# Moving the split hidden activations by 128 bytes against the output weights, on one core

## Chip, cores and metric

One core of a Trainium2 chip runs the whole program in one launch. The metric is the device time of that launch in microseconds. The matrix engine (TensorE) is PE in the profile, the vector engine DVE, the scalar engine ACT, GpSimd POOL, the engine that issues most transfers SP.

## The reference, cut to what matters

256 tokens of width 1024 pass through three blocks one after the other. The first has two layers and the second one layer, each of them with a gated feed-forward before and after a mixer; the third has four layers, each with a mixer and a squared-ReLU feed-forward. All of it is in float32.

```python
def swiglu(x, w_gu, w_down):              # first block; the second is alike, width 2816
    g, u = jnp.split(x @ w_gu, 2, axis=-1)
    return (jax.nn.silu(g) * u) @ w_down

def squared_relu_mlp(xn, w_up, w_down):   # third block, width 4096
    return jnp.square(jax.nn.relu(xn @ w_up)) @ w_down
```

## The kernel before, in words

**Split numbers.** A float32 operand of a matmul is held as two float32r tiles, a high half (a copy that rounds) and a low half (the rest), and a product is three matmuls: high with high, high with low, low with high. ACT makes the high half of each weight unit from its landing buffer (`split_hi`), DVE the low half (`split_lo`), each in rings of two.

**A feed-forward** (class `FeedForward`) goes through its hidden width in units: 22 units of 128 columns in a gated stage (six such stages, 132 units), 16 units of 256 columns in a squared-ReLU stage (four stages, 64 units). For each unit PE runs `_hidden` (weights `in_hi`, `in_lo` stationary, normed activations `feat` moving), and then `_down` of the unit before it: the activations `hid_hi`, `hid_lo` are stationary, 128 columns at a time, and the output weights `down_hi`, `down_lo` move, 512 columns at a time, into four PSUM banks that accumulate over all units. `_down` is three groups: L1302 (`hid_hi` with `down_hi`), L1306 (`hid_hi` with `down_lo`), L1310 (`hid_lo` with `down_hi`), of 4 matmuls each in a gated unit and 8 in a squared-ReLU unit. The last unit of a stage runs the same products by `_last_down` (L1324, L1329, L1334). Every matmul has a weight load of its own. A turn of the loop has two units.

**The mixers** project by `Linear.block` (L1640, L1641, L1645): here `feat` is stationary and the weights `in_hi`, `in_lo` move, 512 columns at a time. Some of their projections (L2173 to L2175, L3110 to L3115) are turned round: weights stationary, `feat` moving, 256 columns.

**Where tiles lie.** `Core.__init__` lays all tiles out in SBUF one after the other. Its helper `phase(name, at)` puts in an unused tile, so that the next address equals `at` modulo `PERIOD` (256 bytes); `NEAR` is 64 bytes. With the address of `in_hi` as origin, the code gives these remainders modulo 256: `in_hi`, `in_lo` and `ring_in` 0; `feat` 0; `feat_near` and `feat2_hi`, `feat2_lo` -64; `proj` -64, and with it the tiles that lie over it: `ring_down`, `hid_hi`, `hid_lo`; `arena` -64, and with it `down_hi`, `down_lo`. Gated stages read the activations at -64 (in four of the six stages; two stages of the second block use rows 258 wide that alternate between -64 and +64). Squared-ReLU stages read `feat` at 0 and have their low weights `in_lo_near` at +64. All chunks inside a tile are whole multiples of 256 bytes apart, but for those wide rows.

I call the remainder of the moving operand's address less that of the stationary operand's the offset of a matmul. Before the change it is 0 for all of `_down`, L1207 too; -64 in L1209, L1210, L1217, L1216; 0 in the projection of the convolution mixer; +64 in the first blocks of the last stick-breaking projection (it reads `feat_near`), and -64 in its turned blocks; 0 in the turned block of the sliding-window mixer.

**The order of the work** is each engine's own list, with semaphores between them; SP loads the next unit into a ring when DVE has made the low half of the unit two before. `proj` itself holds the mixers' projections; attention reads parts of it as a matmul operand (L1816, L2046, L2731).

Of the kernel before, what the change touches and what calls it, by code (L numbers as in the profile page):

```python
# [31 lines left out]
PERIOD = 256  # L32
NEAR = 64
# [109 lines left out]
class Core:  # L143


    def __init__(self, nc, ctx, dram):
        self.nc, self.dram = nc, dram

        def sb(name, *shape):
            return ctx.enter_context(nc.sbuf_tensor(name, [P, *shape], F32))  # L150
# [7 lines left out]
        def phase(name, at):  # L158

            gap = (at - nc.sbuf_base) % PERIOD  # L160
            if gap:
                sb(name, gap // 4)
# [13 lines left out]
        at_in = nc.sbuf_base  # L176
# [8 lines left out]
        self.fold = sb("fold", TT, P)  # L185
        self.minus_half = sb("minus_half", 8)
        self.eps = sb("eps", 8)
        phase("hidden_gap", at_in - NEAR)
        at = nc.sbuf_base
        self.proj = sb("proj", TT, PROJ_COLS)  # L190

# [4525 lines left out]
```

## Time and profile before

| | |
|---|---|
| median of 3 runs | 2865.47 us (2858.51 to 2865.72) |
| the profiled execution | 2865.0 us, its span 2863.2 us |
| PE busy | 2766.1 us, 97% of the span |
| DVE, ACT, POOL busy | 1944.9, 1195.1, 610.4 us |
| mean granted clock | 0.984 |

A matmul's length in the profile holds its latency, and the next one starts before it ends. What a matmul costs in a dense stretch is therefore the distance between two starts, which I call its pitch, and not its length: a row of the timeline gives the start of a run of equal matmuls, and the difference of two starts, divided by the matmuls between them, is the pitch. Starts are rounded to 0.01 us.

### The profile page before, as it was taken

How to read it: one execution, taken by the hardware profiler on the slowest of the kernel's cores; microseconds unless marked ns; L12 is line 12 of the kernel's file. 1: busy time of each engine (PE TensorE's matmuls, PEld its weight loads, DVE VectorE, ACT ScalarE, POOL GpSimd, SP SyncE). 2: the span in 40 equal slices, each digit the busy share in tenths (PEclk: the TensorE clock that was granted, in tenths of full speed). 3: DMA queues.
4: the chain of work that ended last, by engine and by line, in shares of the span. 5: the costliest groups of instructions: out<-in, count | busy, mean ns of one | idle time of the engine just before them, and what ended most of it. 6: DMA issues, size and time to landing. Idle time of an engine off the chain costs nothing.

```text
span 2863.2 us, 43965 instructions
## 1 busy us (share of the span) xinstructions
PE 2766.1 (97%) x17384; PEld 2446.3 (85%) x17384; DVE 1944.9 (68%) x2181; ACT 1195.1 (42%) x1468; POOL 610.4 (21%) x513
## 2 busy tenths in 40 slices
PE   8999999999999999999999999999999989999998
PEld 7987789989978998998789898888788878888887
DVE  7985665678866986664666656666766657665665
ACT  4343443333353343334443445434443444345433
POOL 5953310048533971000100000000000320000000
PEclk9999999999999999999999999999999999999999
DMA  7654135457535674443344343544554335533542
GB/s 288 259 185 158 53 126 191 184 210 255 209 104 186 255 262 176 178 161 103 118 181 178 140 162 155 205 176 154 185 204 176 120 123 215 196 134 119 210 191 105
DMA packets 126465, 500.31 MB, mean 175 GB/s; under 512 B 11024, under 2 KB 12336, under 8 KB 92960
## 3 DMA queue, kind: packets, MB, share of 16 engines
q1 hardware_dynamic: 112768, 450.39, 43.0%
q0 software_dynamic: 13600, 48.60, 4.9%
q8 instruction: 65, 1.06, 0.2%
q14 instruction: 32, 0.26, 0.0%
HBM read 497.90 MB, written 1.05 MB: 174 GB/s over the span
## 4 chain that ended last, share of the span: by engine, by line
PE 74%; DVE 13%; issue 6%; ACT 3%; DMA 2%; POOL 2%; DVEq 0%; SPq 0%; ACTq 0%; POOLq 0%
PE duo L1207 8%; PE duo L1302 7%; PE duo L1306 6%; PE duo L1310 6%; PE duo L1209 6%; PE duo L1210 6%; PE duo L1217 6%; PE duo L1216 4%; DVE down_lo L360 4%; PE duo L1640 3%; PE duo L1641 3%; PE duo L1645 3%; DVE in_lo L360 2%; DVE hid_hi L1466 2%; DMA ring_in<-in_ffn_in 2%
## 5 line engine op out<-in xcount | busy, mean ns | idle before, releaser
L360 DVE TENSOR_TENSOR in_lo<-ring_in,in_hi 128x2048 fp32r<-128x2048 f32 x295 | 704.9, 2390 | 293.4 <-ACT in_hi L353 293.2
L353 ACT CAST in_hi<-ring_in 128x2048 fp32r<-128x2048 f32 (+1 forms) x293 | 554.8, 1894 | 265.1 <-PE duo L1645 137.9
L360 DVE TENSOR_TENSOR down_lo<-ring_down,down_hi 128x1024 fp32r<-128x1024 f32 (+1 forms) x196 | 370.2, 1889 | 29.5 <-ACT down_hi L353 29.5
L353 ACT CAST down_hi<-ring_down 128x1024 fp32r<-128x1024 f32 (+1 forms) x196 | 260.5, 1329 | 45.4 <-PE duo L1310 44.6
L1302 PE MATMUL duo<-down_hi,hid_hi 128*128 128x512 f32 x984 | 258.5, 394 | 10.5 <-DVE hid_hi L1466 9.3
L1209 PE MATMUL duo<-feat,in_hi 128*128 128x256 f32 (+1 forms) x1056 | 258.6, 285 | 5.2 <-ACT in_hi L353 3.4
L1210 PE MATMUL duo<-feat,in_hi 128*128 128x256 f32 (+1 forms) x1056 | 256.4, 283 | 0.0
L1306 PE MATMUL duo<-down_lo,hid_hi 128*128 128x512 f32 x984 | 254.5, 390 | 0.0
L1310 PE MATMUL duo<-down_hi,hid_lo 128*128 128x512 f32 x984 | 253.3, 389 | 0.0
L1207 PE MATMUL duo<-feat,in_hi 128*128 128x512 f32 x1024 | 250.8, 395 | 0.0
L1207 PEld LDWEIGHTS duo<-feat,in_hi 128*128 128x128 f32 x1024 | 191.3, 188 | 46.5 <-DVE feat L655 6.0
L1005 POOL TENSOR_TENSOR small<-small,minus_half 128x1 f32<-128x1 f32 x16 | 8.8, 552 | 1006.3 <-DVE small L1038 1006.0
L1306 PEld LDWEIGHTS duo<-down_lo,hid_hi 128*128 128x128 f32 x984 | 185.3, 188 | 39.8
L1310 PEld LDWEIGHTS duo<-down_hi,hid_lo 128*128 128x128 f32 x984 | 185.0, 188 | 38.6
L1375 ACT ACTIVATE act<-act 128x256 f32<-128x256 f32 x88 | 36.8, 418 | 423.4 <-DVE act L1433 423.3
L1209 PEld LDWEIGHTS duo<-feat,in_hi 128*128 128x128 f32 x1056 | 201.9, 191 | 11.5 <-ACT in_hi L353 3.7
L3312 POOL TENSOR_TENSOR mod_sum<-mod_sum,mod_w 128x1024 f32<-128x1024 f32 x63 | 206.9, 3285 | 5.3
L1302 PEld LDWEIGHTS duo<-down_hi,hid_hi 128*128 128x128 f32 x984 | 172.3, 189 | 39.0 <-ACT down_hi L353 11.0
L1210 PEld LDWEIGHTS duo<-feat,in_hi 128*128 128x128 f32 x1056 | 202.0, 191 | 2.2
L1382 ACT CAST hid_hi<-act 128x512 fp32r<-128x512 f32 x64 | 39.7, 620 | 347.6 <-DVE act L1481 347.6
L1640 PE MATMUL duo<-in_hi,feat 128*128 128x512 f32 x432 | 173.7, 402 | 0.2 <-DVE feat L655 0.2
L1641 PE MATMUL duo<-in_hi,feat 128*128 128x512 f32 x432 | 170.5, 395 | 0.0
(522 smaller groups left out, 5508.2 us busy)
## 6 DMA issues: line engine op xcount, KB each, us to landing
ring_in<-in_ffn_in SPq DMA_DIRECT2D x196, 1024.0 KB, 6.1
ring_down<-in_ffn_down SPq DMA_DIRECT2D x132, 512.0 KB, 3.5
ring_down<-in_ffn_down SPq DMA_DIRECT2D x64, 1024.0 KB, 4.8
mod_w<-in_w_ada POOLq DMA_DIRECT2D x72, 512.0 KB, 4.8
ring_in<-in_sb_w_qkv SPq DMA_DIRECT2D x24, 1024.0 KB, 5.1
ring_in<-in_conv_w_in SPq DMA_DIRECT2D x12, 1024.0 KB, 5.1
ring_in<-in_gla_w_in SPq DMA_DIRECT2D x12, 1024.0 KB, 5.1
ring_in<-in_nsa_w_in SPq DMA_DIRECT2D x10, 1024.0 KB, 5.1
```

The source lines that it names most:

```text
L353: act.copy(hi[:, s, 0:n], raw[:, s, 0:n]).then_inc(hi_ready.sem, 1)
L360: dve.tensor_tensor(lo[:, s, 0:n], raw[:, s, 0:n], hi[:, s, 0:n].bitcast(F32), ALU.subtract).then_inc(lo_ready.sem, 1)
L1207: pe.matmul(out.rearrange("p (s n) -> p s n", s=2), hi, k.feat[:, :, c, :], start=opens, stop=False, skip_group_check=True)
L1209: pe.matmul(out, hi, self.feat_hi[:, c, :], start=opens, stop=False, skip_group_check=True)
L1210: pe.matmul(out, hi, self.feat_lo[:, c, :], start=False, stop=False, skip_group_check=True)
L1217: return pe.matmul(out, lo, self.feat_hi[:, c, :], start=False, stop=(c == KC - 1), skip_group_check=True)
L1302: pe.matmul(self.acc(t, n), hid_hi, down_hi, start=first and ch == 0, stop=False)
L1306: pe.matmul(self.acc(t, n), hid_hi, down_lo, start=False, stop=False)
L1310: last = pe.matmul(self.acc(t, n), hid_lo, down_hi, start=False, stop=False)
L1640: pe.matmul(out, self.feat_hi[:, 4 * h + c, tok], w_hi[:, c, :], start=(h == 0 and c == 0), stop=False)
L1641: pe.matmul(out, self.feat_lo[:, 4 * h + c, tok], w_hi[:, c, :], start=False, stop=False)
L3312: pool.tensor_tensor(total, total, mod.w[:, s, :], ALU.add).then_inc(mod.used.sem, 1)
```

## The change

The unused tile ahead of `proj` is sized so that `proj`, and with it `ring_down`, `hid_hi` and `hid_lo`, lie at +64 instead of -64. The tile ahead of `arena` is still sized for -64, so `down_hi` and `down_lo` keep their remainder. The offset of the matmuls of `_down` and `_last_down` goes from 0 to -128, which modulo 256 is +128. No instruction is added, removed or moved in order.

```diff
         self.fold = sb("fold", TT, P)
         self.minus_half = sb("minus_half", 8)
         self.eps = sb("eps", 8)
-        phase("hidden_gap", at_in - NEAR)
+        phase("hidden_gap", at_in - NEAR + PERIOD // 2)
         at = nc.sbuf_base
         self.proj = sb("proj", TT, PROJ_COLS)
```

## Rows read from the trace of the kernel before

**Rows 1.** The page: span, busy us of each engine, granted TensorE clock in 40 slices:

```profile
span 2863.2 us, 43965 instructions
...
PE 2766.1 (97%) x17384; PEld 2446.3 (85%) x17384; DVE 1944.9 (68%) x2181; ACT 1195.1 (42%) x1468; POOL 610.4 (21%) x513
...
PEclk9999999999999999999999999999999999999999
```

**Rows 2.** The page: chain that ended last, shares of the span by engine:

```profile
PE 74%; DVE 13%; issue 6%; ACT 3%; DMA 2%; POOL 2%; DVEq 0%; SPq 0%; ACTq 0%; POOLq 0%
```

**Rows 3.** PE groups by form: count, busy us, mean ns of one, idle before:

```profile
L1302 PE MATMUL duo<-down_hi,hid_hi 128*128 128x512 f32 x984 | 258.5, 394 | 10.5 <-DVE hid_hi L1466 9.3 <-ACT hid_hi L1382 1.1
...
L1306 PE MATMUL duo<-down_lo,hid_hi 128*128 128x512 f32 x984 | 254.5, 390 | 0.0
...
L1310 PE MATMUL duo<-down_hi,hid_lo 128*128 128x512 f32 x984 | 253.3, 389 | 0.0
...
L1324 PE MATMUL duo<-down_hi,hid_hi 128*128 128x512 f32 x56 | 19.8, 400 | 0.0
...
L1207 PE MATMUL duo<-feat,in_hi 128*128 128x512 f32 x1024 | 250.8, 395 | 0.0
...
L1816 PE MATMUL duo<-arena,proj 128*64 128x256 f32 x112 | 18.7, 413 | 2.1 <-DVE feat L3948 1.5 <-DVE feat L1936 0.7
```

**Rows 4.** Timeline of PE, half a turn of a squared-ReLU stage: start, length, count:

```profile
1801.13 3.83 PE L1207 MATMUL duo<-feat,in_hi 128*128 128x512 f32 x16
...
1804.80 2.05 PE L1216 MATMUL duo<-feat,in_lo 128*128 128x256 f32 x16
...
1806.69 1.99 PE L1302 MATMUL duo<-down_hi,hid_hi 128*128 128x512 f32 x8
...
1808.51 1.98 PE L1306 MATMUL duo<-down_lo,hid_hi 128*128 128x512 f32 x8
...
1812.14 3.83 PE L1207 MATMUL duo<-feat,in_hi 128*128 128x512 f32 x16
```

**Rows 5.** Timeline of PE, half a turn of a gated stage:

```profile
505.05 2.05 PE L1217 MATMUL duo<-feat_hi,in_lo 128*128 128x256 f32 x16
...
506.93 1.09 PE L1302 MATMUL duo<-down_hi,hid_hi 128*128 128x512 f32 x4
...
507.86 1.07 PE L1306 MATMUL duo<-down_lo,hid_hi 128*128 128x512 f32 x4
...
509.68 0.28 PE L1209 MATMUL duo<-feat_hi,in_hi 128*128 128x256 f32 x1
```

**Rows 6.** Timeline of PE, convolution mixer's projection, 12 matmuls apart:

```profile
1948.10 1.07 PE L1645 MATMUL duo<-in_lo,feat 128*128 128x512 f32 x4
...
1950.82 1.07 PE L1645 MATMUL duo<-in_lo,feat 128*128 128x512 f32 x4
```

**Rows 7.** Timeline of PE, last stick-breaking projection, 12 matmuls apart:

```profile
2563.35 1.08 PE L1645 MATMUL duo<-in_lo,feat 128*128 128x512 f32 x4
...
2566.10 1.08 PE L1645 MATMUL duo<-in_lo,feat 128*128 128x512 f32 x4
```

**Rows 8.** Timeline of PE, the first gated stage's first unit:

```profile
25.10 1.98 PE L1217 MATMUL duo<-feat,in_lo 128*128 128x256 f32 x16
...
26.91 1.09 PE L1302 MATMUL duo<-down_hi,hid_hi 128*128 128x512 f32 x4
```

**Rows 9.** Timeline of PE, same projection later, 108 matmuls apart:

```profile
2573.56 0.28 PE L2173 MATMUL duo<-feat,in_hi 128*128 128x256 f32 x1
...
2585.80 0.28 PE L2173 MATMUL duo<-feat,in_hi 128*128 128x256 f32 x1
```

**Rows 10.** Timeline of PE, sliding-window mixer's projection, 7 matmuls apart:

```profile
790.18 0.28 PE L3110 MATMUL duo<-feat,in_hi 128*128 128x256 f32 x1
...
791.02 0.28 PE L3111 MATMUL duo<-feat,in_hi 128*128 128x256 f32 x1
```

**Rows 11.** Timeline of DVE, same half turn as rows 5, idle time in brackets:

```profile
507.13 0.42 DVE L1433 TENSOR_TENSOR act<-duo,y 128x256 f32<-128x256 f32 x1 [2.17 <-PE duo L1217]
```
## What I predict, and why

> **What bounds the kernel now.** I read the page first. PE is busy for 2766.1 of 2863.2 us, DVE for two thirds, and the granted clock is the higher level (2.4 GHz) in nine tenths or more of every slice [rows 1]. The chain of work that ended last lies on PE for 74% [rows 2]; the reader should see that no other engine has a share near it. So PE's own pace sets the time, and an edit that adds no instruction can only act through that pace or through a wait that is not there yet.
>
> The groups by form come next. The products with the output weights are 984 matmuls in each of three groups and 56 more in each of the three groups of the last units, for which L1324 stands [rows 3], so 3 x 984 + 3 x 56 = 3120 matmuls with 512 moving columns. PE was idle ahead of them for 10.5 us in all, nearly all of it for `hid_hi` from DVE [rows 3]. Their mean lengths differ though their forms are the same: 394, 390 and 389 ns in order of execution [rows 3]. That is the first sign that their pace has a history.
>
> Then the timeline, read for pitch. In the squared-ReLU half turn, 8 matmuls L1302 take 1806.69 to 1808.51, 227.5 ns each, and the 16 after them 1808.51 to 1812.14, 226.9 ns each. The 16 of L1207 take 1801.13 to 1804.80, 229.4 each [rows 4]. In the gated half turn 4 matmuls L1302 take 0.93 us, 232.5 ns each, and the 8 after them 1.82 us, 227.5 each [rows 5]. At the higher clock 512 columns alone are 512 / 2.4 = 213.3 ns. The reader should see a floor near 226.7 ns, and that a group entered from another one first pays some extra and then settles at the floor.
>
> What the settled pitch depends on shows in two projections with the same form and the same code. At offset 0 twelve matmuls take 1948.10 to 1950.82, 226.7 ns each [rows 6]. At offset +64 twelve take 2563.35 to 2566.10, 229.2 ns each [rows 7]. The second never reaches the floor. So 64 bytes cost 2.5 ns per matmul with 512 columns. With 256 columns there are three paces: 113.3 ns at offset -64 over 108 matmuls [rows 9] and 113.1 in the first unit [rows 8]; 117.5 ns at the same offset -64 in a gated unit after a `_down` [rows 5]; and 120 ns at offset 0, 0.84 us for 7 [rows 10]. So a pace belongs to an offset and to what ran before. The offset modulo 512 seems not to matter: by the code `down_hi` less `hid_hi` is 256 modulo 512, `in_hi` less `feat` is 0, and both settle at the floor [rows 4, 6].
>
> **The change part by part.**
>
> *Addresses.* From `in_hi` to `hidden_gap` are 59,200 bytes, 64 modulo 256. Before, both unused tiles were 128 bytes. Now `proj` wants +64 and is already there, and it is 24,704 bytes long, 128 modulo 256, so it ends at -64, where `arena` wants to begin. Both unused tiles vanish: `proj` and the tiles over it move down by 128 bytes, `arena` and all behind it by 256, which keeps its remainders.
>
> *What it takes away.* The extras that `_down` pays today until it settles. Gated unit: 4 x 232.5 + 8 x 227.5 = 2750 ns less 12 x 226.7 = 2720, so 30 ns, times 132 units is 4.0 us [rows 5]. Squared-ReLU unit: 8 x 0.8 ns and 16 x 0.2, 10 ns, times 64 is 0.6 us [rows 4]. At most these 4.6 us can be saved in `_down`. L1207, which follows `_down`, pays 16 x 2.7 = 43 ns a unit today, 2.8 us in all; that depends on how `_down` leaves PE, and could go either way.
>
> *What it adds.* A price on each of the 3120 matmuls. The trace has no stretch of such matmuls that I can place at offset 128. Bounds: nothing, if it settles as offset 0 does [rows 6]; and 120 - 113.3 = 6.7 ns, the largest gap between two paces of one form [rows 9, 10]. The nearest row is +64 with 2.5 ns [rows 7]. The offset is twice as far from 0, and 256 columns also show more price with more than one step, so I take twice the price of one step, 5.0 ns, as an estimate. 3120 x 5.0 = 15.6 us; less the 4.6 that this price replaces, 11.0 us. At the bounds: 3120 x 6.7 - 4.6 = +16.3 us, and 0 - 4.6 = -4.6 us. One step's price would give 3120 x 2.5 - 4.6 = +3.2 us.
>
> *What I cost at nothing.* DVE's second subtraction reads `ring_down` and `down_hi`, which now lie 128 apart. What hides it is DVE's idle time before the next instruction, 2.17 us in a gated half turn [rows 11]. If it took longer than that, `hid_hi` would be late, and L1302 is queued behind it. The casts of ACT are hidden in the same way. Attention reads parts of `proj` as operands; L1816 has 112 such matmuls with 256 columns [rows 3], and at 6.7 ns either way these are 0.8 us. I leave that out of the sum and in the range. The transfers are the same in number and size, and `arena` moves by a whole period.
>
> The sum is 2865.0 + 11.0 = 2876.0 us for the profiled execution. Its 2865.0 agrees with the median 2865.5, so the forecast for the median is 2876, which is 0.4% slower.
>
> **The rivals.**
>
> *No effect, or one cheap step.* Offset 128 may settle like 0, or cost what 64 costs: 2860 to 2869 us. For it: offset 0 does settle, and a price that repeats every 128 bytes fits the two 512-column offsets in the trace as well as one that repeats every 256. Against it: nothing in the trace shows such a repeat. The Trainium skill (SBUF — State Buffer, "Who interferes with whom") goes further: PE has two independent read ports, one for the moving operand and one for the weight load, and PE never waits on anyone. By that rule addresses don't matter at all, and the kernel would stay at 2865 us. The trace does not agree: the same form at two offsets has 226.7 and 229.2 ns [rows 6, 7].
>
> *Faster: the hidden products fall into their fast pace.* The 256-column matmuls at -64 have two paces, 113.3 and 117.5 ns [rows 9, 5]. The first unit, which no `_down` precedes, has the fast one [rows 8]; a later unit, entered from a `_down` that had settled, has the slow one [rows 5]. The stretch of rows 9 followed a block at +64 that never settled [rows 7], and was fast. If `_down` at 128 leaves PE as that block did, the four gated stages with 256 columns save 4 x 22 x 48 x 4.2 ns = 17.7 us. With a price of 2.5 ns in `_down` (+3.2) the result is 2865 - 14.5 = 2850 us. With 5.0 ns (+11.0) it is 2858. Against it: one case of an entry is no rule, and at the full 6.7 ns in `_down` (+16.3) it decides nothing any more. The rival wins by over 0.3% only where `_down` pays less than about 4.4 ns: 3120 x 4.4 - 4.6 = 9.1, and 17.7 - 9.1 = 8.6 us.
>
> *Slower by more.* The new exit of `_down` brings the hidden products to the 120 ns pace: 88 x 48 x 2.5 ns = 10.6 us on top, 2887 us. The price of 6.7 ns alone gives 2881.
>
> **How the numbers follow.** A measurement of this kernel can tell about 0.3%, 8.6 us, from no change. My forecast (5 ns, hidden pace kept, 2876) has a chance of 0.36. Slower by more (2881 to 2887 and above) has 0.12. No effect or one cheap step (2860 to 2869) has 0.32, of which 0.10 for addresses that don't matter here at all. The fast hidden pace has 0.20: 0.16 near 2850 and lower, 0.04 near 2858, which is counted as the same. So slower 0.48, same 0.36, faster 0.16. The range for 8 in 10 runs from 2848, which takes in the fast pace with one cheap step, to 2887, the worse exit. The forecast case alone has 2871 to 2881.
>
> **What would show it.** In the changed kernel's timeline, the pitch of L1306 and L1310 settled above 226.7 ns, near 231.7, or cycling as at +64, shows the price; 226.7 refutes it. L1302 no longer dearer than the two behind it shows that the entry's extra was replaced. L1209, L1210 and L1217 still at 117.5 ns shows that the hidden pace was kept; 113.3 is the faster rival, 120 the slower one. L1207 at 229.4 shows its entry unchanged. DVE's and ACT's times per instruction should stay, and PE's idle time ahead of L1302 near 10.5 us; growth there would mean that the cost came through a wait and not through the pace. My forecast is wrong if the price at 128 is not further along from that at 64, or if what follows `_down` changes its pace; both rest on an extrapolation from two offsets, and the sum has nothing better.

## The result, and the profile after

| | before | after |
|---|---|---|
| median of 20 runs each | 2865.59 us (2858.51 to 2875.41) | 2871.84 us (2865.17 to 2877.36) |
| ratio | | 1.0021, 95% interval 1.0014 to 1.0029 |
| profiled execution | 2865.0 us, span 2863.2 | 2869.8 us, span 2868.0 |

The kernel became 0.21% slower. The interval leaves out 1, so this is a real cost, but it is under the 0.3% that the prediction counts as no difference. The instructions stand in the same order on every engine, so the two traces can be laid over each other.

The page of the kernel after, span, busy times, granted clock, and the chain that ended last by engine:

```profile
span 2868.0 us, 43965 instructions
...
PE 2768.1 (97%) x17384; PEld 2434.3 (85%) x17384; DVE 1945.5 (68%) x2181; ACT 1196.8 (42%) x1468; POOL 613.5 (21%) x513
...
PEclk9999999999999999999999999999999999999999
...
PE 71%; DVE 15%; issue 7%; ACT 4%; DMA 2%; POOL 2%; DVEq 0%; SPq 0%; ACTq 0%; POOLq 0%
```

The granted clock is the higher level (2.4 GHz) in nine tenths or more of every slice, as before [rows 1]. That does not clear the clock altogether: its mean differs a little between executions, and the account over all kernels below takes that up. PE's busy time rose by 2.0 us only. The chain says more: PE's share of it fell from 74% [rows 2] to 71%, DVE's rose from 13% to 15%. That suggests that something was gained on PE and something lost to DVE.

The groups of PE by form, after (count, busy us, mean ns, idle before):

```profile
L1302 PE MATMUL duo<-down_hi,hid_hi 128*128 128x512 f32 x984 | 261.5, 397 | 13.5 <-DVE hid_hi L1466 12.4 <-ACT hid_hi L1382 1.0
L1306 PE MATMUL duo<-down_lo,hid_hi 128*128 128x512 f32 x984 | 260.2, 396 | 0.0
L1310 PE MATMUL duo<-down_hi,hid_lo 128*128 128x512 f32 x984 | 259.4, 395 | 0.0
```

Against [rows 3] the three groups of `_down` are 3, 6 and 6 ns longer, and the idle time ahead of L1302 grew from 10.5 to 13.5 us.

The timeline of PE after: a unit of a gated stage with 256 columns (503 to 512 us), a unit that follows a wait (128 to 140), and a unit of a squared-ReLU stage (1815 to 1822):

```profile
128.69 1.98 PE L1217 MATMUL duo<-feat,in_lo 128*128 128x256 f32 x16
...
130.87 1.18 PE L1302 MATMUL duo<-down_hi,hid_hi 128*128 128x512 f32 x4 [0.20 <-DVE hid_hi L1466]
...
137.50 2.05 PE L1217 MATMUL duo<-feat,in_lo 128*128 128x256 f32 x16
139.39 1.09 PE L1302 MATMUL duo<-down_hi,hid_hi 128*128 128x512 f32 x4
...
503.70 1.09 PE L1302 MATMUL duo<-down_hi,hid_hi 128*128 128x512 f32 x4
...
506.49 0.28 PE L1209 MATMUL duo<-feat_hi,in_hi 128*128 128x256 f32 x1
...
510.13 1.98 PE L1217 MATMUL duo<-feat_hi,in_lo 128*128 128x256 f32 x16
511.95 1.09 PE L1302 MATMUL duo<-down_hi,hid_hi 128*128 128x512 f32 x4
...
1815.80 2.02 PE L1302 MATMUL duo<-down_hi,hid_hi 128*128 128x512 f32 x8
...
1821.38 3.83 PE L1207 MATMUL duo<-feat,in_hi 128*128 128x512 f32 x16
```

Three things are to be read here.

1. *`_down` pays and never settles.* Gated: 503.70 to 506.49 are 12 pitches, 232.5 ns each, against 229.2 before [rows 5]. Squared-ReLU: 1815.80 to 1821.38 are 24 pitches, 232.5 ns each, against 227.1 before [rows 4]. That is 1584 x 3.3 + 1536 x 5.4 ns = +13.5 us. (It takes all gated units at the price of those with 256 columns. In the 528 matmuls of the 258-column stages the median pitch went from 227.6 to 233.0 ns, which makes the sum 1.1 us larger.)
2. *The hidden products after it became faster.* 510.13 to 511.95 is 113.8 ns per matmul; it was 117.5 [rows 5]. The 48 hidden products of a unit take 506.49 to 511.95, 5.46 us; with a unit of 8.40 us before, of which `_down` took 2.75, they took 5.65. That is 88 x 0.19 = -16.7 us. The length of the L1217 group shows the pace at a glance: 1.98 us is fast, 2.05 us slow [rows 8, 5].
3. *The fast pace can be lost.* At 130.87 L1302 waits 0.20 us for DVE, and the hidden products behind it are slow: 137.50 to 139.39, 118.1 ns each. The next unit is fast again. In the profiled execution 5 of the first 66 gated units ran slow.

The distance between the starts of two L1310 groups is the length of a unit. Its median for each kind of stage, worked out from all starts of the two timelines:

```
                        units   before   after   difference x units
gated, 256 columns        88     8.40     8.25     -13.2 us
gated, 258 columns        44     8.50     8.56      +2.6 us
squared-ReLU              64    11.01    11.13      +7.7 us
                                              sum   -2.9 us
```

By the median unit of each kind the kernel should have become 2.9 us faster. It became 6.0 us slower, by the ratio. The missing 9 us are not in the pitch of the ordinary unit. The waits of PE, after:

```profile
PE duo L1302 <- DVE hid_hi L1466: 12.4, 11, 2.3
```

Before, this wait had 9.3 us [rows 3]. The timeline of DVE after shows where it comes from, a quiet unit at 513 us and a disturbed one from 621 us on:

```profile
513.59 0.29 DVE L1466 CAST hid_hi<-act 128x256 fp32r<-128x256 f32 x1
...
514.94 2.29 DVE L360 TENSOR_TENSOR in_lo<-ring_in,in_hi 128x2048 fp32r<-128x2048 f32 x1 [0.59 <-ACT in_hi L353]
517.14 1.22 DVE L360 TENSOR_TENSOR down_lo<-ring_down,down_hi 128x1024 fp32r<-128x1024 f32 x1
...
621.96 2.19 DVE L1466 CAST hid_hi<-act 128x256 fp32r<-128x256 f32 x1
...
624.57 3.66 DVE L360 TENSOR_TENSOR in_lo<-ring_in,in_hi 128x2048 fp32r<-128x2048 f32 x1
628.15 3.41 DVE L360 TENSOR_TENSOR down_lo<-ring_down,down_hi 128x1024 fp32r<-128x1024 f32 x1
```

And GpSimd's timeline over the same stretch:

```profile
621.60 2.41 POOL L3312 TENSOR_TENSOR mod_sum<-mod_sum,mod_w 128x1024 f32<-128x1024 f32 x1
...
626.16 4.31 POOL L3312 TENSOR_TENSOR mod_sum<-mod_sum,mod_w 128x1024 f32<-128x1024 f32 x1
```

The cast of 0.29 us takes 2.19 us while GpSimd's addition runs from 621.60 to 624.01. The two subtractions behind it are lengthened as well, DVE has no idle time up to 631.9 us, and the next `hid_hi` comes 1.44 us too late for PE at 635.32. The Trainium skill (SBUF — State Buffer, "Who interferes with whom") says that DVE and GpSimd share a pair of ports, and that the one that comes second is blocked for the other's whole instruction. The times here agree with it: the cast ends at 624.15, just after the addition at 624.01, and the second subtraction at 631.56, about 1.1 us after the next addition at 630.47; 1.22 us is its length alone.

### The profile page after: what moved, and what is told of

The parts are those of the page before. It is cut to its first block, busy times and chain, and to the rows that moved or that the text cites. A ratio compares the mean times of both kernels' runs of the same rounds, so it can differ in the third digit from the quotient of the medians.

```text
span 2868.0 us, 43965 instructions
## 1 busy us (share of the span) xinstructions
PE 2768.1 (97%) x17384; PEld 2434.3 (85%) x17384; DVE 1945.5 (68%) x2181; ACT 1196.8 (42%) x1468; POOL 613.5 (21%) x513
## 4 chain that ended last, share of the span: by engine, by line
PE 71%; DVE 15%; issue 7%; ACT 4%; DMA 2%; POOL 2%; DVEq 0%; SPq 0%; ACTq 0%; POOLq 0%
PE duo L1207 8%; PE duo L1302 6%; PE duo L1306 6%; PE duo L1310 6%; PE duo L1209 5%; PE duo L1210 5%; PE duo L1217 5%; DVE down_lo L360 5%; PE duo L1216 4%; PE duo L1640 3%; PE duo L1641 3%; PE duo L1645 3%; DVE in_lo L360 3%; DVE hid_hi L1466 2%; DMA ring_in<-in_ffn_in 2%
## 5 line engine op out<-in xcount | busy, mean ns | idle before, releaser
L1302 PE MATMUL duo<-down_hi,hid_hi 128*128 128x512 f32 x984 | 261.5, 397 | 13.5 <-DVE hid_hi L1466 12.4
L1306 PE MATMUL duo<-down_lo,hid_hi 128*128 128x512 f32 x984 | 260.2, 396 | 0.0
L1310 PE MATMUL duo<-down_hi,hid_lo 128*128 128x512 f32 x984 | 259.4, 395 | 0.0
L1209 PE MATMUL duo<-feat,in_hi 128*128 128x256 f32 (+1 forms) x1056 | 253.9, 283 | 5.1 <-ACT in_hi L353 3.4
L1210 PE MATMUL duo<-feat,in_hi 128*128 128x256 f32 (+1 forms) x1056 | 251.6, 281 | 0.0
L1207 PE MATMUL duo<-feat,in_hi 128*128 128x512 f32 x1024 | 250.9, 395 | 0.0
L1207 PEld LDWEIGHTS duo<-feat,in_hi 128*128 128x128 f32 x1024 | 191.2, 188 | 47.1 <-DVE feat L655 6.0
L1306 PEld LDWEIGHTS duo<-down_lo,hid_hi 128*128 128x128 f32 x984 | 186.6, 190 | 44.3
L1310 PEld LDWEIGHTS duo<-down_hi,hid_lo 128*128 128x128 f32 x984 | 185.9, 189 | 43.5
L1302 PEld LDWEIGHTS duo<-down_hi,hid_hi 128*128 128x128 f32 x984 | 172.4, 189 | 42.9 <-ACT down_hi L353 13.2
```

Of the source, the lines that this page charges most:

```text
L1207: pe.matmul(out.rearrange("p (s n) -> p s n", s=2), hi, k.feat[:, :, c, :], start=opens, stop=False, skip_group_check=True)
L1209: pe.matmul(out, hi, self.feat_hi[:, c, :], start=opens, stop=False, skip_group_check=True)
L1210: pe.matmul(out, hi, self.feat_lo[:, c, :], start=False, stop=False, skip_group_check=True)
L1302: pe.matmul(self.acc(t, n), hid_hi, down_hi, start=first and ch == 0, stop=False)
L1306: pe.matmul(self.acc(t, n), hid_hi, down_lo, start=False, stop=False)
L1310: last = pe.matmul(self.acc(t, n), hid_lo, down_hi, start=False, stop=False)
```

## The experiments

The kernel before is the base of every kernel and every ratio.

**1. The hid tiles alone.** `ring_down`, `proj` and `arena` stay at their remainders.

```diff
-        at += 4 * RING * UNIT
+        at += 4 * RING * UNIT + PERIOD // 2
```

> Only hid_hi and hid_lo move by 128 bytes; proj, ring_down and arena stay where they were before. Theory (the price comes from the remainder of each matmul's two operands): the same as the full change, ratio 1.001 to 1.003 to the kernel before, L1306 and L1310 at a pitch of about 232 ns, L1209 and L1217 of a gated unit at 113.3. Rival (it comes from the landing ring, the projections or the arena, which moved as well): ratio 1.000, pitches 226.7 and 117.5.

Measured 2869.69 us against 2864.54, ratio 1.0024 (1.0014 to 1.0034). The pitches are those of the change, units of 8.25, 8.56 and 11.13 us too. The whole effect belongs to the tiles that `_down` loads as weights.

**2. Everything but the hid tiles.** The edit of the change, and the hid tiles shifted back.

```diff
-        phase("hidden_gap", at_in - NEAR)
+        phase("hidden_gap", at_in - NEAR + PERIOD // 2)
...
-        at += 4 * RING * UNIT
+        at += 4 * RING * UNIT + PERIOD // 2
```

> The complement: proj and ring_down move by 128 bytes and arena by 256 as in the full change, but hid_hi and hid_lo keep their old remainder against down_hi and down_lo. Theory: ratio 1.000 to the kernel before, pitches 226.7 (L1306, L1310) and 117.5 (L1217), DVE's and ACT's times per instruction as before. Rival (moved landing ring or arena): ratio 1.002.

Measured 2865.21 us, 1.0007 (0.9997 to 1.0017), with the pitches of before. `ring_down`, `proj` and `arena` cost nothing that can be measured.

**3. Only `hid_lo` shifted.** Only the last group of `_down`, L1310, has offset 128.

```diff
-        at += 4 * RING * 2 * TOKENS
+        at += 4 * RING * 2 * TOKENS + PERIOD // 2
```

> Only hid_lo moves by 128 bytes, so of the three groups only L1310, the last before the hidden products, has offset 128. Theory (the hidden products' pace is set by how the last group leaves PE): L1302 and L1306 near the floor of 226.7 ns after their entry, L1310 about 232, hidden products of gated units at 113.3; 1040 matmuls x 5.5 ns = 5.7 us paid, about 14 us of pitch gained, of which waits for DVE take back some: 2855 to 2862 against 2866 before, ratio 0.996 to 0.999. Rival (the pace follows the whole of the product, or hid_hi's place): hidden pace stays 117.5, ratio 1.002.

Measured 2870.57 us, 1.0023 (1.0014 to 1.0031). The timeline of PE, a gated unit and a squared-ReLU unit:

```profile
503.89 2.05 PE L1217 MATMUL duo<-feat_hi,in_lo 128*128 128x256 f32 x16
505.77 1.09 PE L1302 MATMUL duo<-down_hi,hid_hi 128*128 128x512 f32 x4
...
507.62 1.10 PE L1310 MATMUL duo<-down_hi,hid_lo 128*128 128x512 f32 x4
508.55 0.28 PE L1209 MATMUL duo<-feat_hi,in_hi 128*128 128x256 f32 x1
...
1820.43 1.98 PE L1306 MATMUL duo<-down_lo,hid_hi 128*128 128x512 f32 x8
1822.24 2.02 PE L1310 MATMUL duo<-down_hi,hid_lo 128*128 128x512 f32 x8
1824.11 3.82 PE L1207 MATMUL duo<-feat,in_hi 128*128 128x512 f32 x16
```

In the squared-ReLU unit L1310 has 1.87 us / 8 = 233.8 ns, and L1306 just ahead of it 226.3: the price switches with the offset, from one group to the next. But the hidden products stay slow (1.88 us / 16 = 117.5 ns). My theory that the offset of the last group alone decides their pace fell.

**4. Only `hid_hi` shifted.** L1302 and L1306 at 128, L1310 at 0.

```diff
-        at += 4 * RING * UNIT
+        at += 4 * RING * UNIT + PERIOD // 2
...
-        at += 4 * RING * 2 * TOKENS
+        at += 4 * RING * 2 * TOKENS + PERIOD // 2
```

> Only hid_hi moves by 128 bytes: L1302 and L1306 at offset 128, L1310 back at 0. Theory: 2080 matmuls x 5.5 ns = 11.4 us paid, less some 4 us of today's entry, plus a new entry at L1310; L1310 settles at 226.7 and hands over as before, so hidden products stay at 117.5: 2871 to 2877, ratio 1.002 to 1.004. Rival (hid_hi's place sets the hidden pace): 113.3 and a ratio near 1.000.

Measured 2869.88 us, 1.0017 (1.0004 to 1.0030). The timeline of PE:

```profile
505.39 1.09 PE L1310 MATMUL duo<-down_hi,hid_lo 128*128 128x512 f32 x4
506.32 0.28 PE L1209 MATMUL duo<-feat_hi,in_hi 128*128 128x256 f32 x1
...
509.95 1.98 PE L1217 MATMUL duo<-feat_hi,in_lo 128*128 128x256 f32 x16
...
1813.02 1.99 PE L1310 MATMUL duo<-down_hi,hid_lo 128*128 128x512 f32 x8
1814.84 3.83 PE L1207 MATMUL duo<-feat,in_hi 128*128 128x512 f32 x16
```

Here the fast hidden pace is there (L1217 in 1.98 us), though L1310 has the old offset. And L1310 doesn't settle in a gated unit: four matmuls in 0.93 us are 232.5 ns each, at offset 0. With eight of them, in the squared-ReLU unit, the mean is 227.5. So the price is not a property of the offset alone; a group carries on for a few matmuls what the group before it left. The last group's pitch does not tell the pace of the hidden products either: it is 232.5 ns in a gated unit of kernel 3, where they are slow, and of kernel 4, where they are fast. What they inherit from `_down` is thus neither the last offset nor the last pitch, and these two runs don't show what it is.

**5 and 6. Offsets +64 and -64.** This is kernel 5; kernel 6 has `at_in` alone there.

```diff
-        phase("hidden_gap", at_in - NEAR)
+        phase("hidden_gap", at_in + PERIOD // 2)
```

> proj, ring_down and the hidden tiles at +128, so all products with the output weights have offset +64; arena as before. Theory (the price of an offset in these products is that of the same offset in the projections): a pitch that cycles at 229.2 ns on average, 2.5 ns over the floor, 3120 x 2.5 - 4.6 = +3.2 us; if the gated units' hidden products are at 113.3 as after the last stick-breaking block, 10 us or so less, ratio 0.997; if they stay at 117.5, ratio 1.001. Rival (any offset but 0 costs about 5.5 ns here): 1.002 to 1.005.

> The same with offset -64 (hidden tiles at 0). No row of before has it with 512 columns. Theory: the price grows with the distance from 0 either way, so about as at +64: 229 ns, ratio 0.997 to 1.001 by the hidden pace. Rival (it grows in one direction, 0, 64, 128, 192): over 232 ns, 3120 x 7 - 4.6 = +17 us, ratio 1.006 with the hidden pace kept.

+64: 2871.08 us, 1.0018 (1.0006 to 1.0031). -64: 2874.66 us, 1.0033 (1.0021 to 1.0045). The timeline of PE at +64, a gated and a squared-ReLU unit:

```profile
506.04 1.07 PE L1302 MATMUL duo<-down_hi,hid_hi 128*128 128x512 f32 x4
...
508.79 0.28 PE L1209 MATMUL duo<-feat_hi,in_hi 128*128 128x256 f32 x1
...
1812.13 2.03 PE L1302 MATMUL duo<-down_hi,hid_hi 128*128 128x512 f32 x8
...
1817.73 3.81 PE L1207 MATMUL duo<-feat,in_hi 128*128 128x512 f32 x16
```

Gated: 2.75 us / 12 = 229.2 ns, the value of [rows 7]. Squared-ReLU: 5.60 us / 24 = 233.3 ns, with the same form, tiles and offset. So one offset has two paces, and something besides the offset chooses. At -64 it is 233.3 ns in both kinds of stage. Every offset but 0 brings the hidden products to the fast pace in most units (at -64 so many units of the first and the third stage ran slow or waited that their medians are 8.45 us, those of the other two are 8.24). Units at +64 are 8.20, 8.54 and 11.14 us.

**7 and 8. Before and after, with GpSimd's load cut.** GpSimd's multiplication and addition of the modulation weights run on 8 of 1024 columns, so these two kernels leave out nearly all of the modulation sums; transfers and instruction counts are kept.

```diff
-                k.pool_link(pool, pool.tensor_scalar(mod.w[:, s, :], mod.w[:, s, :], k.col("c_2", c), 0.0, ALU.mult, ALU.add))
+                k.pool_link(pool, pool.tensor_scalar(mod.w[:, s, 0:8], mod.w[:, s, 0:8], k.col("c_2", c), 0.0, ALU.mult, ALU.add))
...
-                pool.tensor_tensor(total, total, mod.w[:, s, :], ALU.add).then_inc(mod.used.sem, 1)
+                pool.tensor_tensor(total[:, 0:8], total[:, 0:8], mod.w[:, s, 0:8], ALU.add).then_inc(mod.used.sem, 1)
```

> The kernel before, with GpSimd's multiply and add of the modulation sums done on 8 columns in place of 1024 (so those sums are left out for the rest; transfers and semaphores are kept). DVE then should not be slowed beside it in the gated stages. Reference for the next run: some us faster than the kernel before, about 6 to 12 us, by fewer waits of PE for hid_hi.

> The same cut in the changed kernel (the same part of the modulation sums left out). Theory (the gated stages' faster hidden pace is given back as waits for a slowed DVE): with DVE free the gain shows in full, and the changed kernel is equal to or faster than its partner: 88 x -0.15 + 44 x 0.06 + 64 x 0.12 us = -2.9 us, ratio to the partner 0.998 to 1.000. Rival (the gain is lost elsewhere): still 1.002 to the partner.

Measured 2851.85 us, 0.9948 (0.9936 to 0.9959), and 2851.01 us, 0.9947 (0.9933 to 0.9961). The waits for `hid_hi` of the second one:

```profile
PE duo L1302 <- ACT hid_hi L1382: 1.0, 4, 0.3
```

DVE is gone from the list in both kernels, hardly a unit is longer than the median of its kind (0.2 us in all, against 20.0 us in the kernel after), and the 0.21% between them is gone too: their ratio is 0.9999. The intervals are wide (about 0.2% for the pair), so this supports that the loss needs GpSimd's load, but can't measure the 2.9 us that the pace alone should give. The two traces can: from the first L1310 of each feed-forward stage to its last, summed over the stages, kernel 8 takes 3.1 us less than kernel 7.

**9 to 11. Shift by kind of stage.** A gated unit fills only half of the columns of the hid tiles, so its views can start some columns in. Such a stage then has its own offset while no tile moves. In kernel 9 these are 48 columns, 192 bytes, which makes the offset -192, or +64 modulo 256.

```diff
+        self.hid_at = 3 * NEAR // 4 if silu and not self.shifted else 0
...
-        rows = slice(ch * TOKENS + t * P, ch * TOKENS + (t + 1) * P)
+        rows = slice(self.hid_at + ch * TOKENS + t * P, self.hid_at + ch * TOKENS + (t + 1) * P)
...
-        dve.tensor_tensor(k.hid_lo[:, j, 0:n], whole, hi.bitcast(F32), ALU.subtract).then_inc(k.hid_ready.sem, 1)
+        dve.tensor_tensor(k.hid_lo[:, j, self.hid_at:self.hid_at + n], whole, hi.bitcast(F32), ALU.subtract).then_inc(k.hid_ready.sem, 1)
```

The same slice stands wherever `hid_hi` is written. Kernel 10 has `2 * NEAR // 4` (offset 128) under the same condition. Kernel 11 moves the hid tiles as kernel 1 does and has `2 * NEAR // 4 if silu else 0`, so that only the squared-ReLU stages are at 128.

> Only the four gated stages with 256-column activations read and write their hidden halves 192 bytes further on in the ring slot (offset +64 to the output weights); squared-ReLU stages and the two wide gated stages keep offset 0, and no tile moves. Theory: unit of the narrow gated stages 8.20 us as with +64 everywhere, hidden products at 113.3, all other units as before (8.50, 11.01). 88 x 0.20 = 17.6 us of pitch gained, half of it or more given back to waits for DVE: 2855 to 2861, ratio 0.997 to 0.999, faster than both kernels. Rival (the gated gain is wholly lost to DVE): 1.000.

> The change's offset of 128 in the four narrow gated stages alone. Theory: their unit at 8.25 us as in the full change, the rest as before: 88 x 0.15 = 13.2 us of pitch gained, with half or more given back: ratio 0.998 to 0.9995. Rival (gated stages are slower by the change as well): over 1.000.

> Offset 128 in the four squared-ReLU stages alone (the hidden tiles at +64, the gated stages' views moved back to a remainder of -64); ring_down, proj and arena not moved. Theory: unit at 11.13 us against 11.01, 64 x 0.12 = 7.8 us slower, ratio 1.0027, gated units at 8.40 and 8.50. Rival (most of the loss is in the gated stages): near 1.001.

| | median us | ratio | interval |
|---|---|---|---|
| 9: narrow gated at +64 | 2861.06 | 0.9984 | 0.9971 to 0.9997 |
| 10: narrow gated at 128 | 2863.75 | 0.9985 | 0.9973 to 0.9998 |
| 11: squared-ReLU at 128 | 2872.73 | 1.0026 | 1.0010 to 1.0042 |

The change is thus two opposite effects: -0.15% in the four gated stages with 256 columns, +0.26% in the squared-ReLU stages. With the +0.1% that the wide stages should cost by their units (2.6 us; not run alone) they make +0.2%, the result. Kernels 9 and 10 are faster than both kernels of this case. But neither gains what its units say, 17.6 and 13.2 us.

**12. Kernel 9 with GpSimd's load cut.** It leaves out what kernels 7 and 8 leave out. If waits take all that is missing, the full gain must appear.

> Offset +64 in the narrow gated stages together with the light GpSimd (the same part of the modulation sums left out), to be read against the kernel before with light GpSimd, 0.9948 of the kernel before. Theory (waits for a slowed DVE take back what the pace gains): the 88 x 0.20 = 17.6 us now show in full or nearly, 2834 to 2840 us, 0.9885 to 0.991 of the kernel before, that is 0.994 to 0.996 of its partner. Rival (something else takes the gain back): 0.993 to 0.9945 of the kernel before, as the 5 us seen with GpSimd at its full work.

Measured 2844.51 us (2833.13 to 2851.86), 0.9932 (0.9914 to 0.9951). Against kernel 7, by the two ratios, that is 0.16% or 4.6 us, with an interval of some 6 us either way (7.3 us by the medians, whose bases differ by 1.7), and not 17.6. The theory's 0.9885 to 0.991 lies outside the interval, and the rival's range holds: the waits don't explain what is missing. The timeline of PE in the second gated stage:

```profile
410.75 2.05 PE L1218 MATMUL duo<-feat_hi,in_lo 128*128 128x256 f32 x16
412.63 1.09 PE L1303 MATMUL duo<-down_hi,hid_hi 128*128 128x512 f32 x4
...
414.50 1.10 PE L1311 MATMUL duo<-down_hi,hid_lo 128*128 128x512 f32 x4
```

The hidden products are slow (117.5 ns) and `_down` is dear (1.87 us / 8 = 233.8 ns), through the second and the third stage (44 units, 8.46 us at the median), while the first and the fourth have the fast pair (units of 8.20 us). The second stage of kernel 9 has the fast pair from end to end, the timeline of its PE:

```profile
481.58 1.08 PE L1303 MATMUL duo<-down_hi,hid_hi 128*128 128x512 f32 x4
...
483.41 1.08 PE L1311 MATMUL duo<-down_hi,hid_lo 128*128 128x512 f32 x4
...
487.97 1.98 PE L1218 MATMUL duo<-feat_hi,in_lo 128*128 128x256 f32 x16
489.78 1.07 PE L1303 MATMUL duo<-down_hi,hid_hi 128*128 128x512 f32 x4
```

Same addresses, same order, two states: 228.8 with 113.1 ns, or 233.8 with 117.5. With no wait for DVE to disturb it, PE stayed in the worse one for two stages, which is 44 x 0.26 = 11 us. That is most of the missing amount: the stages of this kernel take 5.6 us less than those of kernel 7 in the traces, as 44 x -0.20 + 44 x 0.06 = -6.2 us says. It may also be the reason for the wide spread of this kernel's runs: two of its executions with the same mean granted clock, 0.986, took 2844.91 us (the profiled one, with two slow stages) and 2833.13 us. Only the first has a trace, so that the other ran with fewer slow stages is not shown. In kernels 9 and 10 too some narrow gated units ran slow or waited, so many that the median of the fourth stage of kernel 9 is 8.41 us, and those of the first and the fourth stage of kernel 10 are 8.44.

**The account over all kernels.** All figures are in us, against the kernel before. Pace is the sum of the differences of unit medians by kind, times their units, as if every unit ran at the median; measured is the ratio times 2865 us, and rest is measured less pace. "Above" is what units longer than the median of their kind hold in excess, in the one profiled execution of each, less the 13.8 us of the kernel before. "Clock" is explained below the table. "Left" is the rest less these two.

```
kernel                     pace    measured   rest    above    clock    left
2  all but hid tiles        0       + 2.0     + 2.0   + 0.6    + 0.7    + 0.7
3  hid_lo alone           + 6.5     + 6.6     + 0.1   - 4.2    + 0.9    + 3.4
11 squared-ReLU at 128    + 7.7     + 7.4     - 0.3   + 0.1    - 0.1    - 0.3
after                     - 2.9     + 6.0     + 8.9   + 6.2    + 1.7    + 1.0
1  hid tiles alone        - 2.9     + 6.9     + 9.8   +10.6    + 0.8    - 1.6
4  hid_hi alone           - 6.6     + 4.9     +11.5   + 6.8    + 0.9    + 3.8
5  +64                    - 7.5     + 5.2     +12.7   + 8.2    + 1.3    + 3.1
6  -64                    - 2.7     + 9.5     +12.2   + 9.5    - 0.1    + 2.8
9  narrow gated +64       -17.6     - 4.6     +13.0   +10.5    + 1.7    + 0.8
10 narrow gated 128       -13.2     - 4.3     + 8.9   + 5.7    + 1.5    + 1.7
```

The split is clear. Where the hidden products keep their slow pace, the pitches explain the time to 2 us, within intervals of some 3 to 5 us either way. Where they become fast, 9 to 13 us are given back, whatever else was moved, and 6 to 11 us of that stand in long units. In the kernel after, 4.8 of its 6.2 us are in units in which PE waits, and 1.5 in units that ran slow without a wait.

The clock is the other part. At the joints between the stages and in the mixers the granted clock falls to the lower level (1.2 GHz) for short stretches. Outside the feed-forward stages these add up to 88 us in the profiled execution of the kernel before, 72 us in that of kernel 1 and 103 us in that of kernel 5. In all 14 traces the time outside the stages is 1180 us plus half of the time at the lower level, to within 4 us. For example, the 1361 matmuls behind the first gated stage, in the kernel before and in kernel 10, whose tiles lie where they lay before (window, its length, busy us of PE, PEld, DVE, ACT and POOL, granted clock, DMA share, GB/s):

```profile
200.00:412.00 212.00, 196.93 (x1361) 164.08 (x1360) 126.37 (x220) 84.59 (x202) 53.59 (x97) 0.95 0.30 98
...
200.00:418.00 218.00, 201.26 (x1361) 169.19 (x1360) 126.21 (x219) 84.44 (x202) 53.57 (x97) 0.93 0.29 95
```

The second takes 6 us more. It has 30 us at the lower level and the first 20, half of which difference is 5 us.

The executions without a trace show it as well. The kernel after took 2865.5 to 2867.9 us in the five with a mean clock of 0.986 or 0.987, and 2873.4 to 2877.4 us in the four with 0.982. Over all kernels 0.001 of the mean clock goes with 2.2 us. The kernel after has a mean of 0.9840 over its executions, the kernel before 0.9848 over the 91 that were measured beside the experiments; these 0.0008 are 1.7 us, the value in the table; those of the numbered kernels are against the executions of the base measured beside them (all are estimates: the mean clock of 6 to 20 executions is itself uncertain by about 0.0005). Whether the change lowers the clock or chance did, the runs don't show.

## Why the prediction came out as it did

The forecast was 2876 us and the measurement 2871.84, inside the 2871 to 2881 given for the likeliest case. But the way there was not the forecast one: two steps failed, in opposite directions, and that the number came out is luck.

- **The price of `_down`.** Right in kind, a little too small. The estimate was 5.0 ns settled and +11.0 us net; the pitch is 232.5 ns, 5.8 over the floor, and the net is +13.5 us. Kernel 11 shows it alone: 64 units x 0.12 = 7.7 us, measured 7.4. It doesn't settle, and it takes the place of the entry's extra, as said.
- **Why 5.0.** "Twice the price of one step" was close by luck. Kernel 5 has 2.5 ns and 6.7 ns at one and the same offset +64, and -64 has 6.7. The price doesn't grow with the distance from 0; the row of [rows 7] showed one of two states.
- **"Hidden pace kept".** This step failed. The four gated stages with 256 columns fell into the fast pace, -16.7 us, by which the time of the likeliest case should have gone to 2859 or, with the measured price, to 2862. The rival had the right effect, the right stages and nearly the right size (17.7 us). Its condition was not exact: in kernel 3 the last group doesn't settle, and the hidden products stay slow.
- **"What I cost at nothing".** This failed too, and gave back a part of the step above: 6.2 us in long units, of which 4.8 in units in which PE waits. The cover of 2.17 us [rows 11] was read in a quiet half turn. In the others it was too small even before the change, which shows in the 9.3 us of waits for DVE [rows 3]. Beside GpSimd a cast takes 2.19 us instead of 0.29 and a subtraction 3.41 instead of 1.22, and there is no cover left. The prediction named the sign of it, the idle time ahead of L1302, which went from 10.5 to 13.5 us. The sum also had no term for the granted clock, which moves single executions by several us.
- **The rival's threshold.** It was to win where `_down` pays less than 4.4 ns. It paid 5.8, so it could not win by over 0.3%; but 17.7 us were counted as if all of it arrived. Kernel 9, where `_down` of the gated stages pays least, gets 4.6 us of 17.6.
- **No effect, one cheap step, addresses that don't matter.** All three are refuted. Kernels 1 and 2 part the tiles; kernel 3 switches the pitch from 226.3 to 233.8 ns between two neighbouring groups of one unit by nothing but an address. The Trainium skill gives PE two independent read ports and says that PE never waits on anyone (SBUF — State Buffer, "Who interferes with whom"). Read as a rule that addresses don't matter, that is not borne out here; whether another engine can hold PE up at its ports, no run here tests.
- **Neighbours.** L1207 keeps its mean length of 395 ns [rows 3], as said. `ring_down`, `proj` and `arena` cost nothing that can be measured, as said (kernel 2, at most 0.17%).

Shown: the price in `_down` by tile and by stage, the gain of the hidden products, and that 9 to 13 us are given back when these are fast. Shown in part: where that goes. Kernels 7 and 8 tie the loss to GpSimd's load, the waits for `hid_hi` grew by 3.1 us, single units or whole stages drop back to the slow pace, and executions with more time at the lower clock are longer. With these the account closes to 4 us, which is within the intervals; but the long units come from one execution of each kernel, and a remainder of that size would not be seen. Also open is what chooses the state when a stage begins. After offset 0 it is always the slow one but for single units, after other offsets mostly the fast one, and kernel 3 with its dear last group is slow. Whether one kernel changes its state between executions is not shown, since only one of each was profiled; the two executions of kernel 12 at one clock, 11.8 us apart, speak for it.

## What to carry to other kernels

When PE's pitch sets the time, read it by group from the starts in the timeline, for each kind of stage, and multiply by the units: here that accounts for an address change within the measurement as long as no wait is near. A median hides the units that ran at another pace, so count those as well, and set the granted clocks of two executions side by side before explaining a few microseconds between them. A gain in pitch on one side of a shared chain is only worth what the next engine can follow, so read the cover in the busiest unit and not in a quiet one. And an alignment that is good for one shape can be bad for another: choose it per stage, by a column offset into the tile, and not for the whole kernel.

## What the runs showed of the hardware that I had not expected

- A 512-column float32r matmul has 226.7 ns at offset 0, 229.2 or 233.3 at +64, 232.5 on average at 128 and 233.3 at -64, with the same instructions.
- A 256-column matmul at one offset has two stable paces, 113.1 and 117.5 ns, and can keep either over dozens of units. After a wait of 0.20 us between them the next unit ran at the other pace.
- Four matmuls at offset 0 don't recover from a group at 128 (232.5 ns each); eight do (227.5 on average).
- Time at the lower clock costs half its length: outside the feed-forward stages the 14 traces have 1180 us plus half of their 72 to 103 us at the lower level, to within 4 us.
